# Expert stage of a two-layer mixer/MoE step: the last two steps of gate/up by column halves, the transposed activations in two PSUM banks with two copies

## The chip, the cores and the metric

The kernel runs on one core of one Trainium2 chip. The metric is the device time of one execution in microseconds (us); lower is better. The engines are TensorE (PE, with its weight loads as PEld), VectorE (DVE), ScalarE (ACT), GpSimd (POOL) and SyncE (SP), which issues nearly all transfers.

## What is computed

Two layers of a diffusion backbone for 128 prompt tokens and 256 sample tokens, all in float32, D_MODEL = 1024. Each layer has a token mixer (convolution, Fourier, windowed and neighbourhood attention, with gates) and then an expert-choice mixture of 16 experts. Only the latter matters here:

```python
def expert_choice_ffn(h, w_router, w_gate, w_up, w_down):
    cap = EC_CAPACITY * L // N_EXPERTS            # 16 prompt slots, 32 sample slots per expert
    aff = jax.nn.softmax((h @ w_router), axis=-1)
    g, idx = lax.top_k(jnp.swapaxes(aff, 1, 2), cap)
    xs = jax.vmap(lambda hb, ib: hb[ib])(h, idx)
    a = jnp.einsum('becd,edf->becf', xs, w_gate)   # 1024 x 1024 per expert
    u = jnp.einsum('becd,edf->becf', xs, w_up)
    y = jnp.einsum('becf,efd->becd', jax.nn.silu(a) * u, w_down) * g[..., None]
    return scatter_add(idx, y)
```

## The kernel before

Of each layer's 16 experts, four make a group (GRP = 4), and a hardware loop runs over the four groups (`Fori(0, NE // GRP)`). An expert has 64 slots (32 for the sample, 32 for the prompt), and these 64 columns are the stationary operand of its products; the weights stream through as the moving operand.

**Gathering.** For a group, TensorE gathers the chosen tokens by a product with a selection matrix (`gather`, tiles `xe0` to `xe7` in PSUM banks 6 and 7), and ScalarE modulates them into XE. Five of the eight gathers stand ahead of the first gate/up product, the others in its middle, with the transposes of the gated selection (tile `pg`, bank 7).

**An expert j.** `gate_up(j)` runs eight steps k over the contraction. In each, both column halves (512 columns) are done in turn, and for each half the gate product (m = 0, PSUM partitions 0 to 63) and the up product (m = 1, partitions 64 to 127). The results lie in banks 0 to 3 (`gu{j}_{half}`). ScalarE makes the SiLU of a half (line 1591), VectorE multiplies by the up part (line 1666) and gives the bank back. `down(j)` then transposes the products in eight pieces into the one bank of tile `at{j}` (lines 1529 and 1532: four pieces for each half, behind a wait for that half). ScalarE copies the whole bank into AT (line 1577), TensorE waits for that copy, and runs eight steps of the down product (line 1543) into bank 4 or 5. ScalarE and VectorE each copy half of the result (lines 1583, 1584, 1656, 1657). After four experts the results are combined by six products (line 1559) and added to X by VectorE.

**Order.** The order of each engine's work is written out by hand. Each PSUM bank has a `full` and a `free` semaphore; `BankTurns.add` gives a tile its turn in a bank, `e_open` makes TensorE wait until all copies of the bank's earlier tiles are made, `e_close` tells that a tile is full, `e_take` waits for that, `e_release` tells that a copy is made, and `e_copied` waits for that.

**Weights.** An expert has six loads of 2 MiB: gate and up, first and second half of the contraction (slots 0 to 3), and down, first half (slot 4) and second half (slots 5 and 6 in turn). SyncE issues the loads of the next expert in this order: gate and up, first half, when the first four steps of `gate_up` are done; gate and up, second half, when `gate_up` is done; down, first half, when four steps of down are done; down, second half, when down is done. TensorE waits for its loads ahead of steps 0 and 4.

After its own work the last expert of a group (j = 3) makes VectorE also build the selection for the next group (`select`, lines 1642 and 1646).

Of the kernel before, what the change touches and what calls it, by code (L numbers as in the profile page):

```python
# [25 lines left out]
ACT = mybir.ActivationFunctionType  # L26
AX_X = mybir.AxisListType.X

P = 128
D = 1024  # L30
KT = D // P
# [108 lines left out]
def build(nc, A):  # L140
    ctx = ExitStack()
    with ctx:
# [379 lines left out]
        for j in range(GRP):  # L522
            for half in range(2):
                E.add(f"gu{j}_{half}", 2 * (j % 2) + half)
            E.add(f"at{j}", 6)
            E.add(f"y{j}", 4 + j % 2, 2)
        for i in range(6):
            E.add(f"cm{i}", i)
# [2 lines left out]
        def e_open(pe, g, name):  # L531
            b, _, copies_before, _ = E.at[name]
            pe.wait_ge(e_free[b], g * E.copies[b] + copies_before + 1)
            return psum[:, b, :]
# [12 lines left out]
        def e_copied(eng, g, name):  # L547
            b, _, copies_before, copies = E.at[name]
            eng.wait_ge(e_free[b], g * E.copies[b] + copies_before + copies + 1)
# [73 lines left out]
        with nc.Fori(0, DEPTH) as l:  # L623
# [790 lines left out]
            with nc.Block() as block:  # L1414
# [45 lines left out]
                def _(pe):  # L1460
# [15 lines left out]
                    with pe.Fori(0, NE // GRP) as g:  # L1476
# [21 lines left out]
                        def gate_up(j):  # L1498

                            pb = [e_open(pe, g, f"gu{j}_{half}") for half in range(2)]  # L1500
                            n_landed = 16 * (j + 1)
                            for k in range(KT):
                                if j == 0 and k == KT // 2:
                                    for kk in range(KT // 2 + 1, KT):
                                        gather(kk)
                                    affinities_t()
                                if k % 4 == 0:
                                    pe.wait_ge(e_land[k // 4], g * 64 + n_landed)
                                    pe.wait_ge(e_land[2 + k // 4], g * 64 + n_landed)
                                if j == 0:  # L1510
                                    e_copied(pe, g, f"xe{k}")
                                for half in range(2):
                                    for m in range(2):
                                        w = e_dst(2 * m + k // 4)
                                        ins = nc.tensor.matmul(pb[half][64 * m:64 * m + 64, :], XE[:, k, j, :],  # L1515
                                                               w[:, k % 4, half * CH:(half + 1) * CH], start=(k == 0), stop=(k == KT - 1))
                                    if k == KT - 1:
                                        e_close(ins, f"gu{j}_{half}")
                                if k == 3:
                                    ins.then_inc(S["e_half"], 1)  # L1520

                        def down(j):
                            ps = e_open(pe, g, f"at{j}")
                            for k in range(KT):
                                if k % 4 == 0:


                                    e_copied(pe, g, f"gu{j}_{k // 4}")
                                    ins = nc.tensor.matmul(ps[:, k * 64:(k + 1) * 64], AA[0:64, k * P:(k + 1) * P],
                                                           ident[0:64, 0:64], start=True, stop=True)  # L1530
                                else:
                                    ins = nc.tensor.transpose(ps[:, k * 64:(k + 1) * 64], AA[0:64, k * P:(k + 1) * P],
                                                              ident[0:64, 0:64])
                            e_close(ins, f"at{j}")
                            ps = e_open(pe, g, f"y{j}")
                            e_copied(pe, g, f"at{j}")
                            for k in range(KT):
                                if k == 0:
                                    pe.wait_ge(e_land[4], g * 64 + 16 * (j + 1))
                                elif k == 4:  # L1540
# [22 lines left out]
                def _(act):  # L1563
# [3 lines left out]
                    with act.Fori(0, NE // GRP) as g:  # L1567
# [5 lines left out]
                        e_release(nc.scalar.activation(PG, ps[:, 0:384].rearrange("p (t n) -> p t n", t=TT), ACT.Copy), "pg")  # L1573

                        def at_copy(j):
                            ps = e_take(act, g, f"at{j}")
                            e_release(nc.scalar.activation(AT.rearrange("p k s -> p (k s)"), ps, ACT.Copy), f"at{j}")  # L1577

                        def y_copy(j):

# [16 lines left out]
                def _(dve):  # L1597
# [53 lines left out]
                    with dve.Fori(0, NE // GRP) as g:  # L1651
# [7 lines left out]
                        for j in range(GRP):  # L1659
                            for half in range(2):  # L1660
                                ps = e_take(dve, g, f"gu{j}_{half}")
                                dve.wait_ge(S["silu_done"], g * 8 + 2 * j + half + 1)
                                if j and half == 0:
                                    e_take(dve, g, f"at{j-1}")
                                cols = slice(half * CH, (half + 1) * CH)
                                e_release(nc.vector.tensor_tensor(AA[0:64, cols], TMP[64:128, cols], ps[64:128, :], ALU.mult),  # L1666
                                          f"gu{j}_{half}")
                            if j == GRP - 1:
                                select(g + 1, g + 2)
                            y_copy(j)  # L1670
# [102 lines left out]
```

## Time and profile before

| | |
|---|---|
| median of 3 runs | 1810.07 us (1804.38 to 1810.22) |
| profiled execution, its own time | 1813.39 us |
| its span | 1811.60 us |
| TensorE busy | 1600.7 us, 88% |
| VectorE, ScalarE, GpSimd busy | 522.1, 490.1, 326.9 us |
| mean granted clock of TensorE | 0.953 of full speed |
| HBM read | 533 MB, 296 GB/s over the span |
| expert stage | about 426 to 912 us (layer 0) and 1314 to 1799 us (layer 1) |

The profile records one execution. A record of a matmul is one pass; a float32 matmul has two, so the 32 matmuls of an expert's gate/up are 64 records, and the 16 of its down product 32 records. In a timeline row, consecutive records of one line are merged: start, length, engine, line, shapes, number of records, and in brackets the idle time ahead of them with what ended it. The two levels of TensorE's clock are 1.2 and 2.4 GHz, and the granted clock gives the mean as a share of the higher.

### The profile page before, as it was taken

The numbers are of one execution on the slowest core, as the hardware profiler recorded it, in microseconds if no ns is written. First come the engines' busy times: TensorE is split into PE (matmuls) and PEld (weight loads), VectorE is DVE, ScalarE is ACT, GpSimd is POOL, SyncE is SP. The second block draws the span as 40 slices with busy tenths as digits, with TensorE's granted clock in tenths as the row PEclk, the third lists the DMA queues.
The fourth block names the chain that finished last, engine by engine and source line by source line (L and its number), as shares of the span: only waits on it lengthen the run. The fifth ranks groups of instructions, "written<-read, shape, count | busy, mean of one in ns | idle before, by whom it ended". The sixth has DMA issues, their size and how long they took to land. (4 is left out here: it accounts for less than half of the span.)

```text
span 1811.6 us, 20641 instructions
## 1 busy us (share of the span) xinstructions
PE 1600.7 (88%) x8165; PEld 961.0 (53%) x8165; DVE 522.1 (29%) x872; ACT 490.1 (27%) x900; POOL 326.9 (18%) x184
## 2 busy tenths in 40 slices
PE   5999999996889889889779999999798898898984
PEld 3988899753333233233259888896443333333331
DVE  3623454332121121021147235442401211212113
ACT  3435543122112121021143455531221211211211
POOL 1644455300000000000035444551000000000000
PEclk8999999997999999999989999999799999999998
DMA  8625434745999999999954434348369999999992
GB/s 353 222 93 175 160 140 155 275 174 200 428 429 397 428 416 417 428 371 429 413 209 165 154 111 167 120 178 325 139 276 428 423 418 428 407 430 428 408 428 95
DMA packets 48618, 536.33 MB, mean 296 GB/s; under 512 B 13200, under 2 KB 13608, under 8 KB 16808
## 3 DMA queue, kind: packets, MB, share of 16 engines
q1 hardware_dynamic: 48552, 535.43, 73.0%
q8 instruction: 44, 0.72, 0.2%
q14 instruction: 22, 0.18, 0.0%
HBM read 533.05 MB, written 2.36 MB: 296 GB/s over the span
## 5 line engine op out<-in xcount | busy, mean ns | idle before, releaser
L1515 PE MATMUL psum<-ring,arena 128*64 128x512 f32 x2048 | 461.9, 605 | 42.9 <-DMA ring<-in_w_e_up 42.8
L791 PE MATMUL psum<-HTH,WSR 128*128 128x384 f32 x1536 | 413.8, 343 | 6.3 <-ACT arena L553 3.7
L1515 PEld LDWEIGHTS psum<-ring,arena 128*64 128x64 f32 x2048 | 155.8, 140 | 334.5 <-issue 333.4
L791 PEld LDWEIGHTS psum<-HTH,WSR 128*128 128x128 f32 x1536 | 280.3, 188 | 23.5 <-issue 18.3
L710 POOL TENSOR_TENSOR WSR<-ring,WSR 128x1024 fp32r<-128x1024 f32 x96 | 233.9, 2437 | 265.7 <-ACT WSR L1024 265.6
L791 PE MATMUL psum<-HTL,WSR 128*128 128x384 f32 x768 | 259.3, 338 | 0.0
L1543 PE MATMUL psum<-ring,arena 128*64 128x512 f32 x768 | 194.9, 662 | 22.0 <-ACT arena L1577 22.0
L1666 DVE TENSOR_TENSOR arena<-arena,psum 64x512 f32<-64x512 f32 x64 | 44.1, 690 | 510.4 <-ACT arena L1591 509.0
L1024 ACT ACTIVATE WSR<-ring 128x1024 fp32r<-128x1024 f32 x96 | 101.6, 1059 | 288.5 <-PE psum L791 288.5
L791 PEld LDWEIGHTS psum<-HTL,WSR 128*128 128x128 f32 x768 | 144.7, 188 | 1.5 <-issue 1.4
L1591 ACT ACTIVATE arena<-psum 64x512 f32<-64x512 f32 x64 | 37.6, 588 | 383.1 <-PE psum L1515 383.1
L1543 PEld LDWEIGHTS psum<-ring,arena 128*64 128x64 f32 x768 | 57.7, 151 | 135.4 <-issue 109.0
L687 POOL MEMSET arena<- 128x888 f32 x2 | 1.7, 838 | 577.3 <-issue 569.8
L1656 DVE COPY arena<-psum 32x512 f32<-32x512 f32 x32 | 21.8, 681 | 284.5 <-PE psum L1543 284.5
L553 ACT ACTIVATE arena<-psum,MOD,SC 128x128 f32<-128x128 f32 (+1 forms) x168 | 65.6, 458 | 132.5 <-PE psum L1482 119.5
L1583 ACT ACTIVATE arena<-psum 32x512 f32<-32x512 f32 x32 | 18.8, 588 | 253.0 <-PE psum L1543 253.0
L998 PE MATMUL psum<-ring,arena 128*128 128x512 f32 x192 | 83.2, 593 | 2.2 <-DMA ring<-in_w_out 2.2
L739 PE MATMUL psum<-ring,condT 128*32 128x512 f32 x384 | 52.5, 676 | 23.0 <-DMA ring<-in_w_ada 12.9
L1313 DVE TENSOR_TENSOR arena<-arena 128x384 f32<-128x384 f32 x48 | 71.9, 1498 | 1.7
L1310 DVE TENSOR_TENSOR arena<-arena,psum 128x384 f32<-128x384 f32 x48 | 26.6, 554 | 139.2 <-ACT arena L1118 121.3
L1246 DVE SCALAR_TENSOR_TENSOR psum<-arena,PRM,psum 128x414 f32<-128x414 f32 x116 | 64.7, 666 | 0.0
L696 POOL TENSOR_TENSOR BWL<-ring,BWH 128x256 fp32r<-128x256 f32 x64 | 60.6, 947 | 20.5 <-ACT BWH L1088 20.5
(187 smaller groups left out, 1489.8 us busy)
## 6 DMA issues: line engine op xcount, KB each, us to landing
ring<-in_w_e_up SPq DMA_DIRECT2D x64, 2048.0 KB, 17.9
ring<-in_w_e_gate SPq DMA_DIRECT2D x64, 2048.0 KB, 13.9
ring<-in_w_e_down SPq DMA_DIRECT2D x48, 2048.0 KB, 16.1
ring<-in_w_ada SPq DMA_DIRECT2D x24, 2048.0 KB, 7.8
ring<-in_w_in SPq DMA_DIRECT2D x24, 2048.0 KB, 7.8
arena<-in_w_e_down SPq DMA_DIRECT2D x16, 2048.0 KB, 18.4
ring<-in_w_branch SPq DMA_DIRECT2D x4, 2048.0 KB, 7.7
ring<-in_w_out SPq DMA_DIRECT2D x4, 2048.0 KB, 7.7
```

Source lines behind the costliest of these rows:

```text
L553: return nc.scalar.activation(dst, src, ACT.Identity, scale=SC[:, which, k, i:i + 1], bias=MOD[:, sec * KT + k, i:i + 1])
L696: nc.gpsimd.tensor_tensor(BWL[:, idx % 2], branch_part_src(idx), BWH[:, idx % 2].bitcast(F32), ALU.subtract).then_inc(S["b_rest"], 1)
L710: nc.gpsimd.tensor_tensor(WSR[:, 1, i % 2], part_src(i), WSR[:, 0, i % 2].bitcast(F32), ALU.subtract).then_inc(S["w_rest"], 1)
L739: ins = nc.tensor.matmul(ps[32 * j:32 * j + 32, :], condT[:, 4 * k2 + j, :], w[:, 4 * k2 + j, :], start=(k2 == 0), stop=(k2 == 1))
L791: ins = nc.tensor.matmul(ps[:, 0:TOK], WSR[:, w, i % 2, k, :], x[:, k, :], start=(k == 0 and w == 0 and x is HTH), stop=(k == KT - 1 and w ...
L998: ins = nc.tensor.matmul(ps[:, :], MRG[:, k, t * P:(t + 1) * P], wo[:, k % 4, half * CH:(half + 1) * CH], start=(k == 0), stop=(k == KT - 1))
L1024: nc.scalar.activation(WSR[:, 0, i % 2], part_src(i), ACT.Copy).then_inc(S["w_high"], 1)
L1246: ins = nc.vector.scalar_tensor_tensor(acc if k < CONV_K - 1 else ACC[:, c, :], U[:, c, k:k + AW], w, acc, ALU.mult, ALU.add)
L1313: nc.vector.tensor_tensor(MRG[:, k, :], MRG[:, k, :], GP[:, idx % 2, :], ALU.add).then_inc(S["gate_add"], 1)
L1515: ins = nc.tensor.matmul(pb[half][64 * m:64 * m + 64, :], XE[:, k, j, :], w[:, k % 4, half * CH:(half + 1) * CH], start=(k == 0), stop=(k ...
L1543: ins = nc.tensor.matmul(ps[64 * half:64 * half + 64, :], AT[:, k, :], e_dst(4 if k < 4 else down_slot(j))[:, k % 4, half * CH:(half + 1) ...
L1666: e_release(nc.vector.tensor_tensor(AA[0:64, cols], TMP[64:128, cols], ps[64:128, :], ALU.mult), f"gu{j}_{half}")
```

## The change

In `gate_up`, steps 0 to 5 stay as they were. Steps 6 and 7 are run for half 0 first and then for half 1. The tile `at{j}` becomes two tiles, `at{j}_0` in bank 6 with the transposes of pieces 0 to 3, and `at{j}_1` in bank 7 with those of pieces 4 to 7. ScalarE copies the first into AT's first half, VectorE the second into the other half. `down` waits for the first copy ahead of step 0 and for the second ahead of step 4.

```diff
--- before.py
+++ after.py
@@ -522,7 +522,8 @@
         for j in range(GRP):
             for half in range(2):
                 E.add(f"gu{j}_{half}", 2 * (j % 2) + half)
-            E.add(f"at{j}", 6)
+            for half in range(2):
+                E.add(f"at{j}_{half}", 6 + half)
             E.add(f"y{j}", 4 + j % 2, 2)
         for i in range(6):
             E.add(f"cm{i}", i)
@@ -1499,7 +1500,7 @@
 
                             pb = [e_open(pe, g, f"gu{j}_{half}") for half in range(2)]
                             n_landed = 16 * (j + 1)
-                            for k in range(KT):
+                            for k, halves in [(k, (0, 1)) for k in range(KT - 2)] + [(k, (half,)) for half in range(2) for k in (KT - 2, KT - 1)]:
                                 if j == 0 and k == KT // 2:
                                     for kk in range(KT // 2 + 1, KT):
                                         gather(kk)
@@ -1507,9 +1508,9 @@
                                 if k % 4 == 0:
                                     pe.wait_ge(e_land[k // 4], g * 64 + n_landed)
                                     pe.wait_ge(e_land[2 + k // 4], g * 64 + n_landed)
-                                if j == 0:
+                                if j == 0 and 0 in halves:
                                     e_copied(pe, g, f"xe{k}")
-                                for half in range(2):
+                                for half in halves:
                                     for m in range(2):
                                         w = e_dst(2 * m + k // 4)
                                         ins = nc.tensor.matmul(pb[half][64 * m:64 * m + 64, :], XE[:, k, j, :],
@@ -1520,21 +1521,22 @@
                                     ins.then_inc(S["e_half"], 1)
 
                         def down(j):
-                            ps = e_open(pe, g, f"at{j}")
+                            for k in range(KT):
+                                at = f"at{j}_{k // 4}"
+                                if k % 4 == 0:
+                                    ps = e_open(pe, g, at).rearrange("p (k s) -> p k s", k=KT)
+                                    e_copied(pe, g, f"gu{j}_{k // 4}")
+                                    ins = nc.tensor.matmul(ps[:, k % 4], AA[0:64, k * P:(k + 1) * P],
+                                                           ident[0:64, 0:64], start=True, stop=True)
+                                else:
+                                    ins = nc.tensor.transpose(ps[:, k % 4], AA[0:64, k * P:(k + 1) * P],
+                                                              ident[0:64, 0:64])
+                                if k % 4 == 3:
+                                    e_close(ins, at)
+                            ps = e_open(pe, g, f"y{j}")
                             for k in range(KT):
                                 if k % 4 == 0:
-
-
-                                    e_copied(pe, g, f"gu{j}_{k // 4}")
-                                    ins = nc.tensor.matmul(ps[:, k * 64:(k + 1) * 64], AA[0:64, k * P:(k + 1) * P],
-                                                           ident[0:64, 0:64], start=True, stop=True)
-                                else:
-                                    ins = nc.tensor.transpose(ps[:, k * 64:(k + 1) * 64], AA[0:64, k * P:(k + 1) * P],
-                                                              ident[0:64, 0:64])
-                            e_close(ins, f"at{j}")
-                            ps = e_open(pe, g, f"y{j}")
-                            e_copied(pe, g, f"at{j}")
-                            for k in range(KT):
+                                    e_copied(pe, g, f"at{j}_{k // 4}")
                                 if k == 0:
                                     pe.wait_ge(e_land[4], g * 64 + 16 * (j + 1))
                                 elif k == 4:
@@ -1573,8 +1575,8 @@
                         e_release(nc.scalar.activation(PG, ps[:, 0:384].rearrange("p (t n) -> p t n", t=TT), ACT.Copy), "pg")
 
                         def at_copy(j):
-                            ps = e_take(act, g, f"at{j}")
-                            e_release(nc.scalar.activation(AT.rearrange("p k s -> p (k s)"), ps, ACT.Copy), f"at{j}")
+                            ps = e_take(act, g, f"at{j}_0").rearrange("p (k s) -> p k s", k=KT)
+                            e_release(nc.scalar.activation(AT[:, 0:KT // 2], ps[:, 0:KT // 2], ACT.Copy), f"at{j}_0")
 
                         def y_copy(j):
 
@@ -1661,10 +1663,12 @@
                                 ps = e_take(dve, g, f"gu{j}_{half}")
                                 dve.wait_ge(S["silu_done"], g * 8 + 2 * j + half + 1)
                                 if j and half == 0:
-                                    e_take(dve, g, f"at{j-1}")
+                                    e_take(dve, g, f"at{j-1}_1")
                                 cols = slice(half * CH, (half + 1) * CH)
                                 e_release(nc.vector.tensor_tensor(AA[0:64, cols], TMP[64:128, cols], ps[64:128, :], ALU.mult),
                                           f"gu{j}_{half}")
+                            ps = e_take(dve, g, f"at{j}_1").rearrange("p (k s) -> p k s", k=KT)
+                            e_release(nc.vector.tensor_copy(AT[:, KT // 2:KT], ps[:, 0:KT // 2]), f"at{j}_1")
                             if j == GRP - 1:
                                 select(g + 1, g + 2)
                             y_copy(j)
```

## Rows read from the trace of the kernel before

**Rows 1.** Page, 40 slices of the span: busy tenths; GB/s of DMA.

```profile
PE   5999999996889889889779999999798898898984
...
DMA  8625434745999999999954434348369999999992
GB/s 353 222 93 175 160 140 155 275 174 200 428 429 397 428 416 417 428 371 429 413 209 165 154 111 167 120 178 325 139 276 428 423 418 428 407 430 428 408 428 95
```

**Rows 2.** TensorE's waits, whole span: total us, times, longest.

```profile
PE psum L1515 <- DMA ring<-in_w_e_up: 42.8, 23, 2.7
...
PE psum L1543 <- ACT arena L1577: 22.0, 32, 0.7
```

**Rows 3.** Windows at a seam: busy of PE, PEld, DVE, ACT, POOL; clock, DMA share, GB/s.

```profile
794.00:796.00 2.00, 2.00 (x12) 0.72 (x10) 0.00 (x0) 0.00 (x0) 0.00 (x0) 1.00 0.60 254
796.00:798.00 2.00, 2.00 (x10) 0.43 (x6) 0.00 (x0) 0.00 (x0) 0.00 (x0) 1.00 0.06 25
```

**Rows 4.** Timeline of SyncE: issues of loads, expert stages.

```profile
554.75 0.33 SPq L1439 DMA_DIRECT2D ring<-in_w_e_gate  x1
...
674.79 0.33 SPq L1439 DMA_DIRECT2D ring<-in_w_e_gate  x1
...
779.86 0.33 SPq L1437 DMA_DIRECT2D arena<-in_w_e_down  x1
...
798.28 0.33 SPq L1439 DMA_DIRECT2D ring<-in_w_e_gate  x1
...
1446.13 0.33 SPq L1439 DMA_DIRECT2D ring<-in_w_e_gate  x1
...
1685.32 0.33 SPq L1439 DMA_DIRECT2D ring<-in_w_e_gate  x1
```

**Rows 5.** Timeline of TensorE around the end of a group, layer 0.

```profile
759.46 8.78 PE L1515 MATMUL psum<-ring,arena 128*64 128x512 f32 x32 [2.70 <-DMA ring<-in_w_e_up]
...
770.95 5.30 PE L1543 MATMUL psum<-ring,arena 128*64 128x512 f32 x16 [0.69 <-ACT arena L1577]
...
781.37 5.39 PE L1559 MATMUL psum<-arena 128*128 128x512 f32 x12 [1.69 <-DVE arena L1657]
```

**Rows 6.** Timeline of TensorE, one expert in the middle of a group.

```profile
608.18 7.09 PE L1515 MATMUL psum<-ring,arena 128*64 128x512 f32 x32 [2.32 <-DMA ring<-in_w_e_up]
...
616.74 0.43 PE L1529 MATMUL psum<-C,arena 64*128 64x64 f32 x2 [0.15 <-DVE arena L1666]
...
618.04 7.09 PE L1543 MATMUL psum<-ring,arena 128*64 128x512 f32 x32 [0.69 <-ACT arena L1577]
```

**Rows 7.** Timeline of the same tail, ScalarE and VectorE.

```profile
614.45 0.59 ACT L1591 ACTIVATE arena<-psum 64x512 f32<-64x512 f32 x1 [14.21 <-PE psum L1515]
...
615.22 1.46 DVE L1666 TENSOR_TENSOR arena<-arena,psum 64x512 f32<-64x512 f32 x2 [14.80 <-ACT arena L1591]
...
615.30 0.59 ACT L1591 ACTIVATE arena<-psum 64x512 f32<-64x512 f32 x1 [0.27 <-PE psum L1515]
...
617.39 0.60 ACT L1577 ACTIVATE arena<-psum 128x512 f32<-128x512 f32 x1 [1.50 <-PE psum L1532]
```

**Rows 8.** Lines by form: copies from PSUM, busy us and mean ns.

```profile
L1573 ACT ACTIVATE arena<-psum 128x384 f32<-128x384 f32 x8 | 3.9, 490 | 5.1 <-PE psum L1490 5.1
...
L1330 DVE COPY XN<-psum 128x256 f32<-128x256 f32 x12 | 5.0, 415 | 0.8 <-PE psum L927 0.8
```

**Rows 9.** Timeline of TensorE: waits for loads, and first down records.

```profile
637.55 7.09 PE L1515 MATMUL psum<-ring,arena 128*64 128x512 f32 x32 [1.15 <-DMA ring<-in_w_e_up]
...
880.96 7.09 PE L1515 MATMUL psum<-ring,arena 128*64 128x512 f32 x32 [2.70 <-DMA ring<-in_w_e_up]
...
890.75 5.13 PE L1543 MATMUL psum<-ring,arena 128*64 128x512 f32 x16 [0.69 <-ACT arena L1577]
...
1768.06 8.52 PE L1515 MATMUL psum<-ring,arena 128*64 128x512 f32 x32 [2.70 <-DMA ring<-in_w_e_up]
...
1779.29 3.65 PE L1543 MATMUL psum<-ring,arena 128*64 128x512 f32 x16 [0.69 <-ACT arena L1577]
```

## The prediction

> **What bounds the kernel now.** I read the slices of the page first. In the two expert stretches the 16 DMA engines are at nine tenths and TensorE wavers between seven and nine; ahead of them TensorE stands at nine and the DMA engines at two to seven [rows 1]. So the experts are paced by their weights. Four experts take 24 loads of 2 MiB, which is 50.3 MB; at the 428 GB/s of a full slice this is 117.6 us. The list of waits agrees: TensorE waited 23 times for the up weights, 42.8 us in all, and 32 times for the copy of the transposed activations, 22.0 us in all [rows 2].
>
> A saving in a kernel paced by loads is worth something only where the loads themselves run dry. The DMA windows around the seam between two groups of four experts show such a place: 254 and then 25 GB/s in two neighbouring stretches of 2 us [rows 3]. SyncE issues nothing between 779.86 and 798.28, since the next pair of slots comes free only when TensorE has done the first half of gate/up of the next group [rows 4]. The distance between the first issues of two groups is 120.04 us (554.75 to 674.79) and 123.49 us (674.79 to 798.28) in layer 0, and 119.6 us on average in layer 1 (two groups from 1446.13 to 1685.32) [rows 4]. Against 117.6 us that is 2.4, 5.9 and 2.0 us without loads.
>
> The PE timeline over this seam gives the chain that sets it. The last wait for a load is at 759.46 (2.70 us). From there to the issue at 798.28 TensorE waits for no load: second half of gate/up, tail, down, combine, gather, gate/up [rows 5]. Hence **a microsecond saved in the tail of the last expert of a group moves the whole load stream; in the other three experts it only lengthens the next wait for loads.** There are three seams in each layer, and behind the fourth group comes the end of the layer, where nothing is loaded that TensorE waits for. So there are 8 tails that count, out of 32.
>
> **The change, part by part.** The tail now, from the timeline of an undisturbed expert [rows 6, 7]: half 0 of gate/up closes, and its SiLU starts at 614.45; half 1 closes later and its SiLU starts at 615.30, ends at 615.89; the two products run 615.22 to 616.68; transposes of half 1 start at 616.74 and are done when ScalarE takes them at 617.39; it copies all 512 columns 617.39 to 617.99; down starts at 618.04. From the last gate/up matmul (608.18 + 7.09 = 615.27) to down it is 2.77 us.
>
> *Order by halves.* The number of matmuls and weight loads is the same. One step of one half is two matmuls, four records, and the two SiLUs start 0.85 us apart [rows 7]: half 0 closes 0.85 us before half 1. With the new order it closes two such pieces before, 1.7 us. So SiLU 0, product 0 and the first four transposes come earlier (they can then follow the last gate/up matmul at 615.3 at once). Half 1 closes when it did, so SiLU 1 stands still. Product 1 is the second of two of 0.69 us that end at 616.68, so it starts at 615.99, 0.10 us behind the end of SiLU 1 at 615.89. It can gain those 0.10 us at most. Steps that follow each other in one bank cost nothing visible: down always accumulates in one bank and has the same 7.09 us for 32 records [rows 6].
>
> *Two banks and two copies.* ScalarE now copies columns of k 0 to 3 after SiLU 1, when the first four transposes are done, so from about 616.0. Its 128x512 copy takes 0.60 us [rows 7] and its 128x384 copy 490 ns, VectorE's 128x256 copy from PSUM 415 ns [rows 8]. I take 0.4 us for either half (bounds: 0.38 by the slope of the two ScalarE rows, 0.6 as the whole copy). So half 0 is there by 616.6 at the worst, before the transposes of half 1 end at 617.3 to 617.4. The copy of half 1 runs beside the first four steps of down, half of 7.09 us. Without that cover it would cost its 0.4 to 0.6 us again. What goes is TensorE's wait for the copy, 0.69 us [rows 6]. I take 0.69 us per tail; 0.79 with the earlier product; 0.60, the length of the copy itself, if what remains of the wait is a hand-over that stays.
>
> The Trainium skill (TensorEngine Tiling (Array Packing), Key Properties) says that changing the tiling mode drains TensorE, and transposes and down use different tilings. No row isolates that drain; a drain would keep part of the 0.69 us; with the lower bound of 0.60 the eight tails below would give 4.8 us.
>
> *Queues.* VectorE's new copy stands before the selection for the next group and before y's copies. In the last expert of a group the selection moves back by about 1 us, beside 7 us of down. ScalarE's shorter copy stands where the old one did. The second wait and semaphore update are free. Bank 7 is free by then: its last copy is made before SiLU 0. SyncE has no new instruction; the loads released by down's fourth step and end come 0.7 us earlier, into a queue that is full.
>
> *Eight tails.* 8 x 0.69 = 5.5 us.
>
> *The clock.* The granted clock falls from the 2.4 to the 1.2 GHz level after some pauses. Down's first 16 take 3.65 us at 1779.29 but 5.30 us at 770.95 and 5.13 us at 890.75 (16 records in each row); a whole down takes 7.09 us warm. Such a fall is in 14 of the 32 downs, which all follow the same 2.77 us tail. In the tails that count it is in five of eight, two of them these, with 1.48 to 1.70 us each, in all 8.2 us [rows 5, 6, 9]. With the change the pause is 2.08 us with transposes in it. Other pauses give the bounds: the 12 waits for loads up to 2.32 us (the one before 608.18) were followed by a fall in no case, and nor was the 1.69 us before each combine; of the 11 waits from 2.49 to 2.71 us seven were, as at 759.46, and four were not, as at 880.96 [rows 5, 6, 9]. A pause of 2.08 us lies among those that cost nothing, so I expect the falls before down to go. Bounds: 8.2 us and nothing.
>
> The Trainium skill (TensorE: Matmul & The Clock Gate, Loop structure matters more than you think) speaks against it from another side: a wait for loads between bursts makes the matmuls behind it run cold, and the other 24 tails only lengthen such waits. By that rule the waits before gate/up, now 2.6 and then 3.3 us, go cold oftener.
>
> That is a cost in front of a full queue: such a fall in the first half of gate/up (as in the one before 637.55, which leaves a wait of only 1.15 us there) is absorbed by the next wait [rows 9].
>
> **The sum.** 5.5 + 8.2 = 13.7 us. Two of these tails, in layer 1, would then save 2.4 us where 2.0 us are dry; spread over its seams I take off 0.2: 13.5. The profiled execution took 1813.39 us (span 1811.60); less 13.5 it is 1799.9. The median, 1810.07, is 3.3 us below it, which I read as two falls of the clock fewer. Taking one of these among the five: 5.5 + 4 x 1.65 = 12.1, and 1810.07 - 12.1 = 1798. I say 1799.
>
> **Rivals.**
> 1. *Only the copy's wait goes.* Falls before down stay, or come back elsewhere in the same chain. 8 x 0.69 us: 1804.5. For it: seven of the falls follow waits for loads, which remain. Against it: the 12 short waits.
> 2. *The load stream hides it all.* Then nothing moves: 1810. For it: full DMA slices. Against it: 2.0 to 5.9 us per group without loads.
> 3. *Slower: cold second halves.* Behind the last wait of a group the second half of gate/up runs cold in three of eight cases, from 759.46 (8.78 us) to 1768.06 (8.52), 1.43 to 1.69 us over 7.09 each [rows 5, 6, 9]. If a new rhythm puts all eight there, five more cost 8.5 us, and with the falls before down unchanged that is -5.5 + 8.5 = +3.0, so 1813. It decides from four more such falls on. Against it: this wait is 2.70 us because two loads land 9.8 us apart and a half lasts 7.09 us; the change lengthens the wait before, not this one.
> 4. *They go too.* A first half that goes cold leaves a wait of 1.15 us before the second, which never fell. Three fewer falls: about 4.7 us more, 1794.
>
> **How the numbers follow.** Forecast 0.50, rival 1 0.27, rival 2 0.08, rival 3 0.05, rival 4 0.10. Half a per cent is 9.05 us, about what a measurement of this kernel can tell from no change; below 1801.0 is faster. The forecast's own range is 1795 to 1803, and I count 0.43 of its 0.50 as faster, with rival 4 and a little of rival 1: 0.56. Slower by over 0.5% would need 1819: 0.03. The rest, 0.41, is within. The range takes in rivals 1 and 4: 1792 to 1807.
>
> **What would show it.** Right: no wait of TensorE for a copy before down; 2.0 to 2.1 us from gate/up to down; ScalarE and VectorE copies of about 0.4 us; first issues of groups 118 to 119 us apart; hardly a down above 7.2 us; waits for up weights grown from 42.8 us to over 60. Wrong: a wait for VectorE's copy at down's fifth step, downs of 8.7 us behind the shorter tail, or group distances unchanged.

## The result, and the profile after

The changed kernel takes 1790.01 us at the median of 4 runs (1788.64 to 1794.19), the kernel before 1807.91 us at the median of 4 (1804.38 to 1810.22). The ratio is 0.9907 with a 95% interval of 0.9885 to 0.9929: faster by 0.9%, that is by 13 to 21 us. The forecast was 1799 us with a range from 1792 to 1807. The direction was right; the gain of 17.9 us was half as large again as the 12.1 us of the sum for the median.

The profiled execution took 1789.33 us, its span 1787.5 us, 24.1 us less than the span before. The two expert stages together (from the first gate/up of a layer to its last combine) went from 943.2 to 924.0 us, 19.2 us less. The other 4.9 us lie in code that the change doesn't touch; over all profiled executions of this study that rest was between 861.8 and 868.4 us, whatever the kernel. So 19.2 us are the change's, in this pair of executions. A fall, here and below, is a stretch in which the granted clock is at its lower level; a half or a down that runs into one, and takes 8.4 us or more instead of 7.09, is called cold.

The slices of the page, answering to [rows 1]. In the expert stages the DMA line no longer has slices at 371 or 397 GB/s; the lowest inner one is 419:

```profile
PE   5999999996889789798779999999797998988984
...
DMA  9625434644999999999964425348369999999992
GB/s 372 211 95 179 156 138 155 266 190 185 428 428 419 429 429 425 429 424 429 398 238 165 150 95 182 116 174 329 141 269 427 428 422 429 425 430 429 427 429 112
```

TensorE's waits, answering to [rows 2] (total us, times, longest). The wait for the copy is gone, the wait for loads has grown from 42.8 to 64.9 us, and what is left in the tails is the wait for the products:

```profile
PE psum L1516 <- DMA ring<-in_w_e_up: 64.9, 32, 3.4
PE psum L1529 <- DVE arena L1668: 30.4, 32, 1.0
```

SyncE's first issues of groups, answering to [rows 4]. They are 117.80 and 117.79 us apart in layer 0, where they were 120.04 and 123.49, and 117.65 in layer 1. I had put the time of 24 loads at 117.6 us: the stream no longer runs dry.

```profile
549.06 0.33 SPq L1440 DMA_DIRECT2D ring<-in_w_e_gate  x1
...
666.86 0.33 SPq L1440 DMA_DIRECT2D ring<-in_w_e_gate  x1
...
784.65 0.33 SPq L1440 DMA_DIRECT2D ring<-in_w_e_gate  x1
...
1428.15 0.33 SPq L1440 DMA_DIRECT2D ring<-in_w_e_gate  x1
...
1545.80 0.33 SPq L1440 DMA_DIRECT2D ring<-in_w_e_gate  x1
```

One tail on TensorE, answering to [rows 6]. Gate/up ends at 602.79 + 7.09 = 609.88, the first transposes follow without a pause, the only wait left is 0.94 us for product 1, and down starts at 611.90, 2.02 us after gate/up (2.77 before; in the last experts of the groups it is 2.01 or 2.02, where it was 2.71). Ends of matmuls are modelled, so a row can overlap the next by some hundredths:

```profile
602.79 7.09 PE L1516 MATMUL psum<-ring,arena 128*64 128x512 f32 x32 [2.71 <-DMA ring<-in_w_e_up]
609.81 0.43 PE L1529 MATMUL psum<-C,arena 64*128 64x64 f32 x2
610.08 0.35 PE L1532 MATMUL psum<-C,arena 64*128 64x64 f32 x3
611.37 0.40 PE L1529 MATMUL psum<-C,arena 64*128 64x64 f32 x2 [0.94 <-DVE arena L1668]
611.62 0.35 PE L1532 MATMUL psum<-C,arena 64*128 64x64 f32 x3
611.90 7.09 PE L1545 MATMUL psum<-ring,arena 128*64 128x512 f32 x32
```

The same tail on ScalarE and VectorE, answering to [rows 7]: SiLU 0 is 1.71 us ahead of SiLU 1 (it was 0.85), ScalarE's copy of 256 columns takes 0.38 us and is done long before down, VectorE's takes 0.42 us beside down's first steps:

```profile
608.20 0.59 ACT L1593 ACTIVATE arena<-psum 64x512 f32<-64x512 f32 x1 [15.02 <-PE psum L1516]
608.82 0.69 DVE L1668 TENSOR_TENSOR arena<-arena,psum 64x512 f32<-64x512 f32 x1 [15.46 <-ACT arena L1593]
...
609.91 0.59 ACT L1593 ACTIVATE arena<-psum 64x512 f32<-64x512 f32 x1 [1.13 <-PE psum L1516]
...
610.53 0.38 ACT L1579 ACTIVATE arena<-psum 128x256 f32<-128x256 f32 x1
610.53 0.69 DVE L1668 TENSOR_TENSOR arena<-arena,psum 64x512 f32<-64x512 f32 x1 [1.03 <-ACT arena L1593]
...
612.00 0.42 DVE L1671 COPY arena<-psum 128x256 f32<-128x256 f32 x1 [0.78 <-PE psum L1532]
```

**The chain of a seam.** One number is read for every kernel from here on: from the start of the second half of gate/up in a group's last expert (behind the last wait for a load) to the first combine product. Before, at the end of group 1 of layer 0 for example, it ran from 637.55 to 657.81, 20.26 us [rows 9 for its start]. It takes only a few values, and the timeline rows tell why:

| the stretch holds | us |
|---|---|
| old tail, clock never falls | 18.52 to 18.57 |
| old tail, one fall (before the second half or before down) | 19.99 to 20.27 |
| old tail, both | 21.76 to 21.91 |
| new tail, clock never falls | 17.69 to 17.73 |
| new tail, one fall (before the second half) | 19.09 to 19.42 |

A layer has four such stretches, a kernel eight. Their sum was 161.5 us before and 141.8 us after. The expert stages less this sum are 781.7 and 782.2 us: all of the gain is in these eight stretches.

### The profile page after: what moved, and what is told of

It is laid out like the page before. It is cut to its first block and busy times, and to the rows that moved or that the text cites. A ratio compares the mean times of both kernels' runs of the same rounds, so it can differ in the third digit from the quotient of the medians.

```text
span 1787.5 us, 20801 instructions
## 1 busy us (share of the span) xinstructions
PE 1570.7 (88%) x8165; PEld 954.9 (53%) x8165; DVE 535.0 (30%) x904; ACT 483.6 (27%) x900; POOL 327.4 (18%) x184
## 5 line engine op out<-in xcount | busy, mean ns | idle before, releaser
L1516 PE MATMUL psum<-ring,arena 128*64 128x512 f32 x2048 | 466.2, 610 | 64.9 <-DMA ring<-in_w_e_up 64.9
L1545 PE MATMUL psum<-ring,arena 128*64 128x512 f32 x768 | 171.9, 596 | 0.0
## 6 DMA issues: line engine op xcount, KB each, us to landing
ring<-in_w_e_up SPq DMA_DIRECT2D x64, 2048.0 KB, 19.2
```

What stands on the lines that cost most here:

```text
L1545: ins = nc.tensor.matmul(ps[64 * half:64 * half + 64, :], AT[:, k, :], e_dst(4 if k < 4 else down_slot(j))[:, k % 4, half * CH:(half + 1) ...
```

## The experiments

Each ran beside the kernel before on the same chip. The table has the ratio to it with its 95% interval, both medians, and from the profiled execution the eight stretches and the falls in them (second half / down), as well as the cold downs among all 32. The kernel before took 1807.9 to 1812.0 us from one group of runs to another, so medians of rows with different neighbours differ by some us for that alone.

| kernel | ratio | median us | kernel before beside it, us | sum of 8 stretches | falls in them | cold downs |
|---|---|---|---|---|---|---|
| before | | 1807.9 |  | 161.5 | 3 / 5 | 14 |
| before, second sample | | one run, 1809.5 | 1808.5 | 158.1 | 3 / 3 | 12 |
| the change | 0.9907 (0.9885 to 0.9929) | 1790.0 | 1807.9 | 141.8 | 0 / 0 | 0 |
| the change, second sample | 0.9913 (0.9890 to 0.9936) | 1792.6 | 1808.5 | 148.6 | 4 / 0 | 0 |
| order only | 0.9978 (0.9962 to 0.9994) | 1808.6 | 1812.0 | 161.2 | 6 / 2 | 10 |
| banks and copies only | 0.9881 (0.9860 to 0.9902) | 1792.6 | 1812.0 | 143.5 | 1 / 0 | 0 |
| last expert of a group only | 0.9917 (0.9892 to 0.9942) | 1799.1 | 1812.0 | 151.6 | 6 / 0 | 6 |
| first three experts only | 0.9985 (0.9967 to 1.0002) | 1808.9 | 1812.0 | 160.9 | 1 / 7 | 7 |
| before, tails filled | 0.9964 (0.9944 to 0.9985) | 1804.2 | 1810.5 | 154.5 | 3 / 0 | 0 |
| before, tails and last wait filled | 0.9963 (0.9940 to 0.9987) | 1804.1 | 1810.5 | 151.0 | 0 / 0 | 0 |
| last expert only, wait filled by 3 | 0.9897 (0.9868 to 0.9926) | 1793.3 | 1810.5 | 145.2 | 0 / 0 | 4 |
| last expert only, wait filled by 1 | 0.9912 (0.9890 to 0.9935) | 1792.5 | 1808.5 | 141.8 | 0 / 0 | 8 |
| the change, wait filled by 3 | 0.9938 (0.9912 to 0.9965) | 1799.3 | 1810.5 | 144.2 | 0 / 0 | 0 |
| the change, wait filled by 1 | 0.9906 (0.9884 to 0.9929) | 1792.1 | 1808.5 | 143.4 | 0 / 0 | 0 |

### Which part of the change does it

**Order only** (e1): steps 6 and 7 by halves, one bank and one copy.

```diff
-                            for k in range(KT):
+                            for k, halves in [(k, (0, 1)) for k in range(KT - 2)] + [(k, (half,)) for half in range(2) for k in (KT - 2, KT - 1)]:
...
-                                for half in range(2):
+                                for half in halves:
```

Expected:

> Only the order of the last two gate/up steps is changed; one bank and one ScalarE copy stay. Theory (the copy's wait and the length of the pause matter): from the last gate/up matmul to down 2.67 to 2.77 us, TensorE still waits 0.69 us for the copy, 10 or more of the 32 downs still start at the lower clock, time 0 to 2 us under before (about 1806 to 1808). Rival (the first four transposes, now straight behind gate/up, break the pause and keep the clock up): the wait for the copy stays but hardly any down is cold, about 8 us less than before (1800).

Measured: from gate/up to down 2.70 to 2.79 us, ten cold downs, and the copy waited for as before. The timeline of TensorE at a tail:

```profile
632.40 8.58 PE L1515 MATMUL psum<-ring,arena 128*64 128x512 f32 x32 [2.70 <-DMA ring<-in_w_e_up]
640.91 0.43 PE L1529 MATMUL psum<-C,arena 64*128 64x64 f32 x2
...
642.38 0.43 PE L1529 MATMUL psum<-C,arena 64*128 64x64 f32 x2 [0.85 <-DVE arena L1666]
...
643.69 3.65 PE L1543 MATMUL psum<-ring,arena 128*64 128x512 f32 x16 [0.69 <-ACT arena L1577]
```

The transposes straight behind gate/up don't keep the clock: the rival falls. The eight stretches are as long as before (161.2 us). The ratio still says 0.1 to 0.4% faster, 4 us in the middle, more than the 0 to 2 us expected; its profile shows no source for that, and it stays open.

**Banks and copies only** (e2): the old order of gate/up.

```diff
-            E.add(f"at{j}", 6)
+            for half in range(2):
+                E.add(f"at{j}_{half}", 6 + half)
...
-                            ps = e_take(act, g, f"at{j}")
-                            e_release(nc.scalar.activation(AT.rearrange("p k s -> p (k s)"), ps, ACT.Copy), f"at{j}")
+                                ps = e_take(act, g, f"at{j}_0").rearrange("p (k s) -> p k s", k=KT)
+                                e_release(nc.scalar.activation(AT[:, 0:KT // 2], ps[:, 0:KT // 2], ACT.Copy), f"at{j}_0")
...
+                                ps = e_take(dve, g, f"at{j}_1").rearrange("p (k s) -> p k s", k=KT)
+                                e_release(nc.vector.tensor_copy(AT[:, KT // 2:KT], ps[:, 0:KT // 2]), f"at{j}_1")
```

Expected:

> Only the two banks and the two copies; the old order of gate/up stays. Theory: the whole gain is here. Tail 2.0 to 2.1 us, no wait for a copy before down, no cold down, time within 2 us of the full change (1788 to 1793). Rival (the order carries part of it through an earlier ScalarE copy or a broken pause): the copy of half 0 arrives late, tail 2.3 us or more, or some downs stay cold; time 1795 or more.

Measured: tails of 2.01 to 2.04 us, no cold down, ratio 0.9881, which overlaps that of the full change. So the whole gain is in the two banks and copies, as far as these runs can tell. The order by halves adds nothing that can be measured: with it or without it the tail is 2.01 to 2.04 us, since in both the second product is what TensorE waits for last.

### Which tails count

**Last expert only** (e3) and **first three only** (e4): both parts, in the one case behind `j == 3`, in the other behind `j < 3`.

```diff
-            E.add(f"at{j}", 6)
+            if j == 3:
+                for half in range(2):
+                    E.add(f"at{j}_{half}", 6 + half)
+            else:
+                E.add(f"at{j}", 6)
```

Expected of the last only:

> The full change for the last expert of each group alone (8 of 32 tails). Theory (only tails between the last wait for a load and the next group's first issue count): nearly the whole gain, 1789 to 1795, though the other 24 tails keep their 2.77 us and their cold downs. Rival (each tail counts by its share): a quarter of the gain, about 4.5 us, 1803.

Expected of the first three only:

> The full change for the first three experts of each group alone (24 of 32 tails). Theory: TensorE's waits for loads grow by the 0.75 us a tail, the time stays within 3 us of before (1805 to 1810). Rival (each tail counts by its share): three quarters of the gain, 13 us, 1795. A second rival (the cold second halves of the last expert vanish because the waits ahead of its first half grow): about 5 us less than before, 1803, with no second half of a last expert at the lower clock.

Measured: with 8 of 32 tails changed 0.9917, with the other 24 changed 0.9985. The load waits of the latter did grow, to 62.4 us. So 8 tails carry nearly all and 24 nearly nothing, as in the forecast. But the last only, at 1799.1 us, misses its range (1789 to 1795). Some of that is the kernel before, which took 1812.0 us there, and its ratio's interval overlaps that of the change; still, five of its six runs are longer than all six of banks and copies only, made beside it. Its profile shows a likely cause: no cold down in the last experts, yet six of eight second halves cold, as here (8.78 us instead of 7.09, and the stretch to the combine is 651.83 - 632.41 = 19.42 us):

```profile
632.41 8.78 PE L1519 MATMUL psum<-ring,arena 128*64 128x512 f32 x32 [2.70 <-DMA ring<-in_w_e_up]
...
643.21 3.65 PE L1553 MATMUL psum<-ring,arena 128*64 128x512 f32 x16
...
651.83 5.39 PE L1569 MATMUL psum<-arena 128*128 128x512 f32 x12 [1.53 <-issue]
```

With the first three only, seven of the eight last downs were cold and only one second half:

```profile
634.11 7.09 PE L1519 MATMUL psum<-ring,arena 128*64 128x512 f32 x32 [2.71 <-DMA ring<-in_w_e_up]
...
644.02 5.12 PE L1553 MATMUL psum<-ring,arena 128*64 128x512 f32 x16 [0.73 <-issue]
```

The second rival of that run (the longer waits take the fall away from the second halves) did happen, but it saved nothing, since the fall then came before down. From these two profiles I took it that nearly every seam has one fall, which goes from before down to before the second half when the tail is shorter; the theory in the next expectation rests on that.

All profiles counted together, those below included, say otherwise. The second half lies ahead of its tail in time, so a fall there can spare down. It mostly did: in the four profiles with the old tail in the last expert and nothing filled (before, its second sample, order only, first three only), down was cold behind 2 of 13 cold second halves and behind 15 of 19 warm ones. But taking away the falls before down didn't bring more cold second halves: these four profiles have 13 in 32 stretches, and the five without a cold down in any (the change, its second sample, banks only, last only, tails filled) have 14 in 40. Six of eight cold second halves are also what order only has, with its old tails. So the falls before down are saved, and how many second halves are cold, from 0 to 6 of 8, differs from profile to profile for a reason that no run here shows.

### The clock without the shorter tail

**Tails filled** (e5) and **tails and last wait filled** (e6). To the kernel before come matmuls whose result nothing reads: one ahead of the wait for product 0 and one ahead of the wait for the copy, and in e6 three more ahead of the wait for the load at step 4 of the last expert. They write into bank 7, so ahead of each tail TensorE first waits that the copy of `pg` in that bank is made.

```diff
+                        def warm(n):
+                            for _ in range(n):
+                                nc.tensor.matmul(psum[0:64, 7, :], C[:, 0:64], C[:, 0:CH], start=True, stop=True)
...
+                                if k == 4 and j == GRP - 1:
+                                    warm(3)
...
+                            e_copied(pe, g, "pg")
...
+                                    if k == 0:
+                                        warm(1)
                                     e_copied(pe, g, f"gu{j}_{k // 4}")
...
+                            warm(1)
                             e_copied(pe, g, f"at{j}")
```

Expected of the tails filled:

> The kernel before, with two further matmuls of 512 columns in each tail whose result nothing reads (one ahead of the wait for the first product, one ahead of the wait for the copy): they fill the pause and do not shorten it. Tail still 2.7 to 2.8 us, no cold down. Theory now (in each seam the clock falls about once, and if not before down then before the second half of the last expert's gate/up, as in the kernel with the last tail alone): some 6 of 8 second halves are cold, and the time is 2 to 5 us under before (about 1807). Rival (as I predicted: the falls before down are simply saved): 3 of 8 second halves cold as before, 8 us less, 1802.

Expected of both filled:

> As the former, with three further unread matmuls also ahead of the wait for the load at step 4 of the last expert. Tail 2.7 to 2.8 us, no cold down and no cold second half in a last expert. If the clock is worth 1.65 us in each of 8 seams: 13 us less than before, 1797 to 1800, and 6 to 7 us above the full change (8 tails of 0.75 us). If the shorter tail is what counts and the clock little: 1806 or more.

Measured: no cold down in either, tails of 2.71 to 2.79 us in both. With the tails filled, the stretches sum to 154.5 us, 7 less than before: five falls fewer. Three second halves were cold, which is the rival's number, not my six, and agrees with falls before down that are simply saved; the ratio 0.9964 (about 6.5 us less than the kernel before on that chip) lies between my 2 to 5 us and the rival's 8. With both filled no fall was left in the stretches and six of them took 18.67 or 18.68 us, about the length of an old tail without a fall. The timeline:

```profile
629.35 2.74 PE L1500 MATMUL psum<-C 128*64 128x512 f32 x6
632.25 7.09 PE L1521 MATMUL psum<-ring,arena 128*64 128x512 f32 x32 [0.16 <-DMA ring<-in_w_e_up]
...
642.06 3.74 PE L1553 MATMUL psum<-ring,arena 128*64 128x512 f32 x16
...
650.93 5.39 PE L1569 MATMUL psum<-arena 128*128 128x512 f32 x12 [1.70 <-DVE arena L1667]
```

The other two took 19.48 and 19.49 us: an unread matmul alone in the array takes 0.86 us, so three of them last 2.6 us, and behind a cold first half the wait is only 1.0 to 1.3 us, so they run into the second half. The profiled execution took 1799.35 us, within the 1797 to 1800 expected, but the median of 12 was 1804.1 us, outside. So the filled version doesn't reach in most executions what its profile shows. The granted clock of the runs goes with their time: the three of 1799.35 to 1799.67 us had 0.971 or 0.972, the nine of 1800.79 to 1815.23 us had 0.964 to 0.970. The longer ones spent more time at the lower clock; in which products, no trace shows. At best the clock alone is worth the 10.5 us by which the stretches shrank (161.5 to 151.0), and the timed runs confirm 2 to 11 us of it.

### What the last expert alone lacked

**Last only, wait filled by 3** (e7) and **by 1** (e11): `warm(3)` or `warm(1)` at the place shown above, in the kernel of e3.

> The full change for the last expert of each group alone, plus the three unread matmuls ahead of the wait at step 4 there. Theory (what the change of the last tail alone lacked was only the six cold second halves): none cold, 7 to 9 us less than that kernel, 1790 to 1793, as the full change. Rival (the other 24 tails are worth something of their own): it stays 4 us or more above the full change.

> The full change for the last expert alone, with one unread matmul (0.86 us) instead of three ahead of the wait at step 4 there, so that it fits into a wait of 1.0 us and leaves a pause of 1.8 us of one of 2.7. Theory (pauses under 2.1 us cost no clock, and the overrun of 0.8 us is gone): none of the last experts' second halves cold, all eight stretches 17.7 us, and 1 to 3 us less than with three such matmuls, about 1791. Rival (one such matmul doesn't keep the clock): 4 or more cold, about 1799 as with none.

Measured: no cold second half in a last expert in either. With three, 1793.3 us, 5.7 us less than with none (7 to 9 expected), though the profiled execution took 1802.08 us. Its stretches take 17.72 to 18.54 us, the longer ones with unread matmuls that overran the wait, and the expert stages less the stretches 787.1 us, where all other profiles have 781.4 to 784.7. Two of the third experts had one fall in the second half and one in down, and behind them the wait ahead of the last expert was gone. So a fall outside the stretches is free only as long as a wait for loads behind it can take it up. With one, 1792.5 us, all eight stretches 17.72 or 17.73 us, and the shortest stages of the study (923.2 us), though 24 tails have their old length and eight downs are cold among them:

```profile
628.66 1.02 PE L1504 MATMUL psum<-C 128*64 128x512 f32 x2
631.56 7.09 PE L1525 MATMUL psum<-ring,arena 128*64 128x512 f32 x32 [1.88 <-DMA ring<-in_w_e_up]
...
649.28 5.39 PE L1575 MATMUL psum<-arena 128*128 128x512 f32 x12 [1.53 <-issue]
```

So the 24 other tails are worth nothing of their own that these runs can tell, and the wait of 1.88 us cost no clock in eight cases of eight, where that of 2.70 us cost it in six of eight. The theory that no pause under 2.1 us costs clock doesn't hold: a first half was cold behind a load wait of 2.04 us in the profile of the change and behind one of 2.01 us in that of the change with the wait filled by 1. The ratio, 0.9912, can't be told from the 0.9917 with nothing filled; only the medians and the stretches say that the filled wait gives something.

### Luck or lasting

**Both kernels once more** (e9, e10), unchanged.

> The kernel before once more, for a second sample of where its clock falls. Theory (one fall in nearly every seam, before down or before the second half of the last expert's gate/up): 7 to 9 falls in the eight stretches from the last wait for a load to the combine; each stretch 18.56, 20.26 or 21.91 us long. Rival (8 was chance): 4 or fewer.

> The full change once more. Theory (the longer waits ahead of the last expert's first half take the fall on themselves, so it misses the second): 0 to 2 falls in the eight stretches, no cold down, 1788 to 1794. Rival (the 0 of the first sample was luck): 3 or more cold second halves of a last expert, and 1794 or more.

Measured: six falls in the stretches of the kernel before, three of each kind (I had expected seven to nine). In the changed kernel four, all before second halves, none before down:

```profile
621.10 7.09 PE L1516 MATMUL psum<-ring,arena 128*64 128x512 f32 x32 [1.83 <-DMA ring<-in_w_e_up]
630.89 8.79 PE L1516 MATMUL psum<-ring,arena 128*64 128x512 f32 x32 [2.71 <-DMA ring<-in_w_e_up]
```

The rival is right about the falls: the zero of the first profile was luck. Its 1794 us is not reached by the median (1792.6), though that profiled execution took 1795.42 us.

**The change, wait filled by 3** (e8) and **by 1** (e12), as a candidate for a better kernel.

> The full change with the three unread matmuls ahead of the wait at step 4 of the last expert. The full change had no cold second half there, the kernel with the banks alone one. Theory: at most one fall is left to save, 0 to 2 us less than the full change, 1788 to 1792. Rival (the unread matmuls overrun a wait of 1.0 us by 0.3 us, where the first half was cold): no gain or 1 us more.

> The full change with one unread matmul ahead of the wait at step 4 of the last expert. Theory: all eight stretches 17.7 us in every execution, so no slower than the full change, at most 2 us faster at the median, and with a narrower spread. Rival (the matmul disturbs as the three did): 2 us or more slower than the full change.

Measured: with three, 0.9938 and 1799.3 us, outside what either the theory or the rival expected; it loses part of the gain. Three of its eight stretches have an overrun of 0.8 us, which explains 2.4 us and not all of the 7 us to the other samples. With one, 0.9906, the same as the change, six stretches at 17.72 or 17.73 us and two with an overrun (18.49 and 18.52), where the first half ahead was so long at the lower clock that it took 9.93 and 10.06 us and no wait was left. So "all eight 17.7 us in every execution" was wrong. The spread (1786.5 to 1794.3) is no narrower than that of the change (1788.8 to 1796.4 beside it). No version beats the change by more than can be measured.

## Why the prediction was wrong in size

**Only eight tails count.** Right. Eight changed tails give 0.9917, 24 give 0.9985, and with one filled wait the eight (1792.5 us) give what all 32 give beside them (1792.6).

**The tail.** Right. I took 0.69 us with 0.60 to 0.79 as bounds. The third expert's tail, the one I had read, became 0.75 us shorter, but in the last experts, which count, it went from 2.71 us to 2.01 or 2.02, which is 0.69 us. What I missed is the other end of the chain: TensorE's pause before the combine went from 1.68 to 1.53 us, in every kernel with a second bank for some expert, even where the last expert kept one bank (first three only; its last tails took 2.82 us). So a stretch without falls is 0.84 us shorter (18.56 to 17.72), and eight of them give 6.7 us instead of 5.5. The hand-over from VectorE's last copy to the combine shrank by those 0.15 us; nothing was tried on why.

**Down runs warm.** Right: 14 and 12 of 32 downs were cold before, none of 64 in the two samples of the change, none of 32 with the banks alone, and none of the 208 downs behind a new tail in all profiles. For the tail, the pauses of up to 2.32 us in the trace of before were the right rows, since it behaved like them. As a rule for every pause they would be wrong: the first halves that were cold behind load waits of 2.04 and 2.01 us, and two second halves behind 2.27 and 2.29 us in the last only filled by 1, are below that mark. The new tail has transposes in it, and its longest idle stretch is 0.9 to 1.0 us.

**The step that failed** is the size of the clock's term in the sum, "In the tails that count it is in five of eight [...] in all 8.2 us": it counts the falls before down alone, and leaves the three cold second halves in the stretches as they were. In the profiled execution after, all eight falls were gone: 161.5 - 141.8 = 19.7 us in the stretches, of which 6.7 are tails and 13.0 the clock, 1.63 us a fall. The sum had 13.5 (13.7 before the 0.2 taken off): 4.8 of the 6.2 us between are the three second halves, 1.2 the pause before the combine, the rest the 0.2. The mechanism behind the term is right, since no down was cold again. That the second halves were warm too was luck of this execution, by what the second samples show: there second halves went from 3 to 4 and downs from 3 to 0. Over both samples of either kernel the falls in the stretches went from 7 to 2 on average, worth 8.2 us. That is the term's own size, but two executions of each, with second halves at 3 and 3 and then 0 and 4, don't settle an average.

**From the profiled execution to the median.** I took off one fall because the median lay 3.3 us under the profiled time, and came to 12.1 us. With the tails at 6.7 us and five falls fewer at 1.63 the gain is 14.9 us, inside the measured 13 to 21 us. The rest up to 17 us can't be told from the spread of the falls and of the code around. And of the 9 us between 1799 and 1790.0, 2.2 are the kernel before itself, whose median was 1810.07 us over 3 runs and is 1807.91 over 4.

**Rivals.** The first (only the copy's wait goes) is refuted by the warm downs, and its other half, that the falls come back in the same chain, by the counts of second halves, 14 in 40 against 13 in 32. The second (the load stream hides it) is right for 24 tails and wrong for eight. The third (cold second halves) has its picture in the kernel with the last tail alone, six of eight, but not its price: it was still faster, and order only has the same six. The fourth (the second halves go too), at 0.10, is what the first profile of the change shows. Its reason accounts for half of it: four of the eight first halves there were cold and left waits of 1.00 to 1.12 us. The other four waits were 2.69 to 2.72 us and cost nothing this time; in the second sample four of six such waits did.

**The rule of the skill on waits for loads.** The Trainium skill (TensorE: Matmul & The Clock Gate, Loop structure matters more than you think) lets matmuls run cold behind a long wait for loads; here it is put to waits of 2 to 3.4 us. The trace agrees in part: waits for loads grew to 64.9 us, and three first halves of last experts were cold behind waits of 3.4 us, which the next wait took up. But down went warm, so the cold halves and downs of all 32 experts didn't become more: 21 before and 9 after, 18 and 12 in the second samples. The next wait can't always take it up: in the profile of the first three only, three first halves took 9.9 to 10.0 us and left no wait before the second.

## What to carry to other kernels

In a stage paced by loads, find the stretch between the last wait for a load and the next issue, and count only what lies in it. A pause in TensorE's work can be paid twice, by its own length and by a fall of the clock behind it, so shortening it from 2.7 to 2.0 us gave more than 0.7 us here. But where other long pauses stay in the same stretch, count the falls of several executions before giving them a price: one profile had none of them, the next four. And when an experiment seems to move a fall from one place to another, count both places over all profiles before believing it. When two parts of a change are made together, ask which of them ends last: here the order by halves never did.

## What was not expected of the hardware

- Of pauses of the same length, 2.70 us, some let the granted clock fall and some don't, and it differs from one execution to the next: in the first sample of the changed kernel none of the eight last second halves ran cold, in the second four.
- A shorter pause can do it too. In the first sample of the change a first half is cold behind a load wait of 2.04 us (8.78 us instead of 7.09), while in the same profile seven waits of 2.69 to 2.76 us cost nothing:

```profile
1618.83 8.78 PE L1516 MATMUL psum<-ring,arena 128*64 128x512 f32 x32 [2.04 <-DMA ring<-in_w_e_up]
```

- TensorE goes from transposes to products in another tiling with no idle time that the trace records (611.62 + 0.35 to 611.90, with modelled ends). The drain on a change of tiling mode that the Trainium skill (TensorEngine Tiling (Array Packing), Key Properties) names, and that the prediction let keep part of the 0.69 us, isn't visible here: the tails that count shrank by all of the 0.69 us.
- A 512-column float32 matmul alone takes 0.86 us (six records in 2.74 us with the last one's end), while two in different column halves of the array share that time: 32 records, 16 matmuls, in 7.09 us.
